# One stage for the parameters, the input norm, the modulation rows and the low-rank inputs, with the row products in four column tiles

## Chip, cores and metric

The kernel runs on one core of one Trainium2 chip. The metric is device microseconds (us) of one execution. TensorE is written PE, VectorE DVE, ScalarE ACT, GpSimd POOL, SyncE SP. A suffix q (SPq) is an engine's own queue of instructions that issue DMAs.

## What is computed

One block with a WKV branch, a state-space branch, a merge and an expert layer. Only its beginning is touched by the change. Cut to that, the reference is:

```python
mod_x = (jax.nn.silu(c) @ w_mod[l] + b_mod[l])[:, None, :]          # w_mod: 2048 x 12288
mod_c = (jax.nn.silu(c_ctx) @ w_mod[l] + b_mod[l])[None, None, :]
sh1x, sc1x, g1x, sh2x, sc2x, g2x = jnp.split(mod_x, N_MOD, axis=-1)
...
hx = rms_norm(x, norm_pre1[l]) * (1.0 + sc1x) + sh1x                # x, ctx: 256 x 2048 each
hc = rms_norm(ctx, norm_pre1[l]) * (1.0 + sc1c) + sh1c
rw_x, z_x, xbc_x, dt_x, gate_x = jnp.split(hx @ w_in[l], IN_SPLITS, axis=-1)
...
# last 640 columns of rw_x, rw_c, after the token shift:
r, k, v, wd_f, wd_b, ad_f, ad_b, gd = jnp.split(slab, RW_SPLITS, axis=-1)   # 96, 96, 96, 96, 256
# used as tanh(wd) @ w2, ad @ a2, sigmoid(gd) @ g2 in the WKV branch
```

Only the first 4096 of the 12288 modulation columns (shift and scale of the first norm) are made in this part; a later stage, which the change leaves alone, makes the rest. All numbers are float32.

## The kernel before

Everything here is laid out with 128 channels on the partitions (P = 128, KC = 16 chunks of channels) and 512 tokens on the free axis (256 of the context, then 256 of x). The order of the work is written out by hand, engine by engine, with semaphores between them. Each stage is a block that all engines enter and leave together. Ahead of the first pair of heads four stages stand one behind the other:

1. setup (lines 166 to 309). SP loads the modulation weights `w_mod_ring`, 8 blocks of 512 columns, 4 MB each, into two buffers. ACT issues 22 small loads of all vectors (`raw`), which PE transposes into `par`. PE then makes one row of 512 modulation values after the other: 16 products (one for each chunk k) with the 128 x 2 `silu_c` as weights and 512 columns of w_mod as the moving side (line 300). So 2 of the array's 128 columns are in use. ACT copies the 2 x 512 row out, PE turns it with 4 small products (line 292, `turn_rows`), and DVE adds the bias (line 271).
2. norm_in (322 to 374). SP loads the token rows (4 x 1 MB), ACT squares them, POOL makes the reciprocal root, DVE scales the rows (line 356), PE transposes them (64 transposes, line 373), and DVE applies gain and shift on the way out of PSUM (line 362), which makes `hT`.
3. lora (380 to 467). SP loads the 5 MB of low-rank input weights `w_lora`. PE runs 6 parts after each other, each over 16 chunks (line 414): 64 products of 96 x 512 and 32 of 128 x 256. ACT and DVE shift each part and apply tanh or sigmoid.
4. The head of rwkv (506 on). SP loads the first weights of the pair loop (`low_rank`, `weights`, `gate_weights`, lines 583 to 596). POOL makes the masks (lines 627 to 652), and ACT, DVE and PE wait for the last of them before the loop over the 16 pairs of heads.

A float32 product stands in the trace as two MATMUL records. The product whose four small ones at a time write partitions 32r to 32r + 31 of one bank (line 1027, in `level_x`) exists in the pair loop:

```python
last = mm(ps[blk(r), 5, q * P:(q + 1) * P], XTc[:, q, blk(r)], F[:, q, r, :], start=True, stop=True)
```

Of the kernel before, what the change touches and what calls it, by code (L numbers as in the profile page):

```python
# [14 lines left out]
ALU = mybir.AluOpType  # L15
# [33 lines left out]
DECAY = -0.6065306597126334  # L49

# [74 lines left out]
def hybrid_block(nc, a, out):  # L125
# [4 lines left out]
    with ExitStack() as whole:  # L130
# [18 lines left out]
        minus_half = sb("minus_half", [P, 1])  # L149
# [16 lines left out]
def setup(nc, sb, sem, ps, a, rows, tiles, ident, ones, head_ones, head_mean, tri, below, minus_half, par, silu_c, modT):  # L166

    with ExitStack() as stage:
        raw = sb("raw", [P, tiles + 1, P], ctx=stage)
        skip = sb("skip", [KC, 2], ctx=stage)  # L170
        sig_c = sb("sig_c", [P, KC, 2], ctx=stage)
        w = sb("w_mod_ring", [P, 2, KC, 512], ctx=stage)
        mod_row = sb("mod_row", [2, 2, 512], ctx=stage)
        consts = sem("consts")
        raw_clear, raw_in = sem("raw_clear"), sem("raw_in")
        w_in = [sem("w_mod_in0"), sem("w_mod_in1")]
        par_tr, par_done, c_sig, c_done = sem("par_tr"), sem("par_done"), sem("c_sig"), sem("c_done")
        skip_done = sem("skip_done")
        row_mm, row_copied, row_tr, mod_done = sem("row_mm"), sem("row_copied"), sem("row_tr"), sem("mod_done")
        w_mod = a["w_mod"].rearrange("l (k p) n -> (l p) k n", p=P)  # L180
        BLOCKS = 2 * D // 512
# [9 lines left out]
        with nc.Block() as block:  # L191

            @block.gpsimd
            def _(pool):
# [12 lines left out]
                const(nc.gpsimd.memset(minus_half[:, :], -0.5))  # L207
                const(nc.gpsimd.memset(ident[:, :], 0.0))
                sel(ident[:, :], ALU.not_equal, 1.0, 0, 1, [[-1, P]])
                const(nc.gpsimd.memset(ones[:, :], 1.0))  # L210
                for t, v in ((head_ones, 1.0), (head_mean, 1.0 / HEAD)):
                    const(nc.gpsimd.memset(t[:, :], 0.0))
                    const(nc.gpsimd.memset(t[0:HEAD, 0:HEAD], v))
                    const(nc.gpsimd.memset(t[HEAD:P, HEAD:P], v))
# [8 lines left out]
                CONSTS[0] = count[0]  # L223

            @block.sync
            def _(sp):
                for n in range(2):
                    sp.dma_start(w[:, n, :, :], w_mod[:, :, n * 512:(n + 1) * 512]).then_inc(w_in[n], 16)
                with sp.Fori(1, BLOCKS // 2) as i:
                    for n in range(2):  # L230
                        sp.wait_ge(row_mm, i * 2 + n - 1)
                        sp.dma_start(w[:, n, :, :],
                                     w_mod[:, :, ds(i * 1024 + n * 512, 512)]).then_inc(w_in[n], 16)

            @block.scalar
            def _(act):
                act.dma_start(skip[:, :], a["ssm_d"].rearrange("l (j e) -> (l j) e", e=2)).then_inc(raw_in, 16)
                act.wait_ge(raw_clear, 1)
                for tile, row, k, width, src in pieces:
                    act.dma_start(raw[row:row + k, tile, 0:width], src).then_inc(raw_in, 16)  # L240
                act.wait_ge(par_done, 2)
                c0 = rows["c"][0]
                for e in range(2):
                    nc.scalar.activation(sig_c[:, :, e], par[:, c0 + e * KC:c0 + (e + 1) * KC],
                                         ACT.Sigmoid).then_inc(c_sig, 1)
                with act.Fori(0, BLOCKS // 2) as i:
                    for n in range(2):
                        act.wait_ge(row_mm, i * 2 + n + 1)
                        nc.scalar.activation(mod_row[:, n, :], ps[0:2, n, :], ACT.Copy).then_inc(row_copied, 1)

            @block.vector
            def _(dve):
# [4 lines left out]
                for half in range(2):  # L257
                    lo, hi = half * 4, min(tiles + 1, half * 4 + 4)
                    dve.wait_ge(par_tr, hi)
                    nc.vector.tensor_copy(par[:, lo * P:hi * P], ps[:, 2 + half, 0:(hi - lo) * P]).then_inc(par_done, 1)  # L260
                dve.wait_ge(c_sig, 2)
                c0 = rows["c"][0]
                for e in range(2):
                    nc.vector.tensor_tensor(silu_c[:, :, e], sig_c[:, :, e], par[:, c0 + e * KC:c0 + (e + 1) * KC],
                                            ALU.mult).then_inc(c_done, 1)
                b0 = rows["b_mod"][0]
                dve.sem_inc(mod_done, 2)
                with dve.Fori(0, BLOCKS // 2) as i:
                    for n in range(2):
                        dve.wait_ge(row_tr, i * 2 + n + 1)  # L270
                        nc.vector.tensor_tensor(
                            modT[:, ds(i * 8 + n * 4, 4), :],
                            ps[:, 4 + n, 0:8].rearrange("p (j e) -> p j e", e=2),
                            par[:, ds(i * 8 + b0 + n * 4, 4)].unsqueeze(2).broadcast_to([P, 4, 2]),
                            ALU.add).then_inc(mod_done, 1)

            @block.tensor
            def _(pe):
                pe.wait_ge(consts, CONSTS[0])
                pe.wait_ge(raw_in, 16 * (len(pieces) + 1))  # L280
                pe.wait_ge(skip_done, 2)
                for t in range(tiles + 1):
                    nc.tensor.transpose(ps[:, 2 + t // 4, (t % 4) * P:(t % 4 + 1) * P], raw[:, t, :],
                                        ident[:, :]).then_inc(par_tr, 1)
                pe.wait_ge(c_done, 2)

                def turn_rows(count, n, guard):

                    pe.wait_ge(row_copied, count + 1)
                    pe.wait_ge(mod_done, guard)  # L290
                    for j in range(4):
                        last = nc.tensor.matmul(ps[:, 4 + n, 2 * j:2 * j + 2], mod_row[:, n, j * P:(j + 1) * P],
                                                ident[0:2, 0:2], start=True, stop=True)
                    last.then_inc(row_tr, 1)

                with pe.Fori(0, BLOCKS // 2) as i:
                    for n in range(2):
                        pe.wait_ge(w_in[n], i * 16 + 16)
                        for k in range(KC):
                            last = nc.tensor.matmul(ps[0:2, n, :], silu_c[:, k, :], w[:, n, k, :],  # L300
                                                    start=(k == 0), stop=(k == KC - 1))
                        last.then_inc(row_mm, 1)
                    for n in range(2):
                        turn_rows(i * 2 + n, n, i * 2 + 2)


CONSTS = [0]


def norm_in(nc, sb, sem, ps, a, ident, minus_half, par, col, modT, hT):  # L310

    with ExitStack() as stage:
        rows = sb("in_rows", [P, NT, D], ctx=stage)
        junk = sb("in_sq", [P, D], ctx=stage)
        ssq = sb("in_ssq", [P, NT], ctx=stage)
        rstd = sb("in_rstd", [P, NT], ctx=stage)
        gain = sb("in_gain", [P, KC, 2], ctx=stage)
        rows_in = [sem(f"rows_in{t}") for t in range(NT)]
        sq_done, rstd_done, gain_done, scaled, turned, h_done = (
            sem(x) for x in ("in_sq_done", "in_rstd_done", "in_gain_done", "in_scaled", "in_turned", "h_done"))  # L320
        srcs = [a["ctx"], a["ctx"], a["x"], a["x"]]
        with nc.Block() as block:

            @block.sync
            def _(sp):
                for t in range(NT):
                    lo = (t % 2) * P
                    sp.dma_start(rows[:, t, :], srcs[t][0, lo:lo + P, :]).then_inc(rows_in[t], 16)

            @block.scalar  # L330
            def _(act):
                for t in range(NT):
                    act.wait_ge(rows_in[t], 16)
                    if t:
                        act.wait_ge(sq_done, t)
                    nc.scalar.activation(junk[:, :], rows[:, t, :], ACT.Square,
                                         accum_out=ssq[:, t:t + 1]).then_inc(sq_done, 1)

            @block.gpsimd
            def _(pool):  # L340
                pool.wait_ge(sq_done, NT)
# [1963 lines left out]
```

## Time and profile before

| | us |
|---|---|
| median of 3 runs | 4772.31 (4768.56 to 4774.83) |
| the profiled execution | 4772.08 |
| its span, first to last instruction | 4770.3 |
| start of the pair loop on PE in it | 297.3 |

The span is shorter than the execution's time by 1.8 us, which lie around it. In the page, a stage is found by its line numbers; in the view of stretches the busy time of an engine is set against the length of the stretch. The mean granted TensorE clock over the span is 0.941 of 2.4 GHz; in a stretch, 1.00 is the upper level and 0.50 the lower (1.2 GHz).

### The profile page before, as it was taken

How to read it: one execution, taken by the hardware profiler on the slowest of the kernel's cores; microseconds unless marked ns; L12 is line 12 of the kernel's file. 1: busy time of each engine (PE TensorE's matmuls, PEld its weight loads, DVE VectorE, ACT ScalarE, POOL GpSimd, SP SyncE). 2: the span in 40 equal slices, each digit the busy share in tenths (PEclk: the TensorE clock that was granted, in tenths of full speed). 3: DMA queues.
4: the chain of work that ended last, by engine and by line, in shares of the span. 5: the costliest groups of instructions: out<-in, count | busy, mean ns of one | idle time of the engine just before them, and what ended most of it. 6: DMA issues, size and time to landing. Idle time of an engine off the chain costs nothing. (4 is left out here: it accounts for less than half of the span.)

```text
span 4770.3 us, 83752 instructions
## 1 busy us (share of the span) xinstructions
PE 4007.9 (84%) x36046; PEld 2453.1 (51%) x36046; DVE 2054.1 (43%) x3479; ACT 732.9 (15%) x1295; POOL 801.7 (17%) x740
## 2 busy tenths in 40 slices
PE   8679999999999967898987999988477777777777
PEld 2246666666666654555655888877332222222233
DVE  0224555555555443656665000011455555545542
ACT  0013222222222211111111000011011011011101
POOL 0020000000000000000100000000354454444441
PEclk9889999999999978889988999999799999999999
DMA  7211111111111105545563443414499999999996
GB/s 270 93 50 42 42 44 43 42 44 43 42 44 43 31 10 158 169 123 149 150 180 100 155 169 143 158 71 150 173 404 400 422 406 406 404 422 402 400 422 260
DMA packets 378768, 868.13 MB, mean 182 GB/s; under 512 B 16300, under 2 KB 211454, under 8 KB 311806
## 3 DMA queue, kind: packets, MB, share of 16 engines
q0 software_dynamic: 73728, 536.90, 27.4%
q1 hardware_dynamic: 303872, 326.74, 22.0%
q8 instruction: 239, 3.92, 0.4%
q10 hardware_dynamic: 894, 0.29, 0.0%
q14 instruction: 35, 0.29, 0.0%
HBM read 859.68 MB, written 4.19 MB: 181 GB/s over the span
## 5 line engine op out<-in xcount | busy, mean ns | idle before, releaser
L2266 PE MATMUL ps<-vb,diag 128*128 128x512 f32 x2048 | 969.8, 621 | 378.5 <-DMA vb<-in_peer_v,ixv 278.8
L2266 PEld LDWEIGHTS ps<-vb,diag 128*128 128x128 f32 x2048 | 384.3, 196 | 964.0 <-issue 606.7
L2168 DVE SCALAR_TENSOR_TENSOR junk<-ub,hT 128x2048 f32<-128x2048 f32 x256 | 586.8, 2292 | 570.4 <-DMA ub<-in_peer_u,ixu 567.9
L945 PE MATMUL ps<-hT,w_pair 128*128 128x512 f32 (+1 forms) x1536 | 661.7, 549 | 37.0 <-POOL id L652 29.8
L1627 PE MATMUL ps<-hT,w_group 128*128 128x512 f32 (+1 forms) x1024 | 404.9, 559 | 19.3 <-DMA w_group<-in_w_in 19.3
L2071 POOL DMA_INDIRECT vb<-in_peer_v,ixv x256 | 311.9, 1218 | 523.4 <-PE ps L2266 485.0
L945 PEld LDWEIGHTS ps<-hT,w_pair 128*128 128x128 f32 x1536 | 261.5, 190 | 189.7 <-issue 130.7
L2063 POOL DMA_INDIRECT ub<-in_peer_u,ixu x256 | 309.0, 1207 | 200.6 <-issue 96.9
L1627 PEld LDWEIGHTS ps<-hT,w_group 128*128 128x128 f32 x1024 | 201.3, 197 | 220.5 <-issue 214.3
L2234 ACT ACTIVATE diag<-ident,coef 128x128 f32<-128x128 f32 x256 | 101.0, 400 | 1007.1 <-PE ps L2266 997.0
L1541 DVE SCALAR_TENSOR_TENSOR mod_by_row<-w_mod_piece,silu_c,mod_by_row 128x512 f32<-128x512 f32 x240 | 187.0, 779 | 114.6 <-DMA w_mod_piece<-in_w_mod 108.9
L1755 PE MATMUL ps<-hT,w_merge 128*128 128x256 f32 x1024 | 223.2, 381 | 14.5 <-DMA w_merge<-in_w_in 14.5
L660 POOL TENSOR_TENSOR bonus<-Kh 128x256 f32<-128x256 f32 x16 | 11.7, 732 | 1223.5 <-DVE Kh L881 1223.5
L1755 PEld LDWEIGHTS ps<-hT,w_merge 128*128 128x128 f32 x1024 | 195.5, 191 | 41.3 <-issue 14.5
L791 DVE SCALAR_TENSOR_TENSOR Ct<-ps,em,Ct 128x64 f32<-128x64 f32 x448 | 106.3, 279 | 185.8 <-PE ps L1044 185.7
L811 DVE TENSOR_TENSOR F<-ps,off 128x1024 f32<-128x1024 f32 x128 | 150.6, 1218 | 61.2 <-PE ps L1019 61.2
L1827 DVE TENSOR_TENSOR sga<-sga,ps 128x1024 f32<-128x1024 f32 x4 | 4.9, 1220 | 339.4 <-PE ps L1755 339.4
L1044 PEld LDWEIGHTS ps<-Ct,Mt 64*64 64x64 f32 x1792 | 73.2, 140 | 116.8 <-issue 87.9
L1454 POOL TENSOR_TENSOR xw<-xt,hd 128x256 f32<-128x256 f32 x48 | 39.6, 857 | 547.9 <-ACT xt L1485 547.9
L1044 PE MATMUL ps<-Ct,Mt 64*64 64x64 f32 x1792 | 104.9, 238 | 13.3 <-DVE Ct L791 13.3
L1936 PE MATMUL ps<-yaT,w_q 128*128 128x256 f32 x512 | 112.5, 383 | 3.3 <-DMA w_q<-in_peer_wq 3.3
L1755 PE MATMUL ps<-mT,w_merge 128*128 128x256 f32 x512 | 112.5, 383 | 2.7 <-DVE mT L1832 2.7
(373 smaller groups left out, 4900.2 us busy)
## 6 DMA issues: line engine op xcount, KB each, us to landing
w_mod_piece<-in_w_mod SPq DMA_DIRECT2D x128, 512.0 KB, 3.8
w_pair<-in_w_in SPq DMA_DIRECT2D x48, 1024.0 KB, 6.0
w_mod_ring<-in_w_mod SPq DMA_DIRECT2D x8, 4096.0 KB, 13.1
w_group<-in_w_in SPq DMA_DIRECT2D x32, 1024.0 KB, 10.6
w_merge<-in_w_in SPq DMA_DIRECT2D x8, 4096.0 KB, 13.2
w_z<-in_w_in SPq DMA_DIRECT2D x8, 2048.0 KB, 13.2
w_merge<-in_w_branch_a SPq DMA_DIRECT2D x4, 4096.0 KB, 13.2
w_merge<-in_w_branch_b SPq DMA_DIRECT2D x4, 4096.0 KB, 13.4
```

The lines of the kernel that those rows point to most:

```text
L791: stt(state(d, c), ps[:, 6, d * HEAD:(d + 1) * HEAD], em[:, z % 2, d, c:c + 1], state(d, c), ALU.mult, ALU.add).then_inc(*VD.did(f"c{j}_{d}"))
L811: tt(F[:, 2 * d:2 * d + 2, :, :], ps[:, 0:4, d * SEQ:(d + 1) * SEQ].rearrange("p r (h c) -> p h r c", h=2), off[:, l - 1, d, :].unsqueeze( ...
L945: last = mm(ps[:, 4, t0:TOK], w[:, m % 2, k, :], hT[:, k, t0:TOK], start=(k == 0), stop=(k == KC - 1))
L1044: last = mm(ps[hs, 6, d * HEAD:(d + 1) * HEAD], m, state(d, before(d, c))[hs, :], start=True, stop=True)
L1541: nc.vector.scalar_tensor_tensor(by_row[:, b, :], part, silu_c[:, k, 0:1], by_row[:, b, :], ALU.mult, ALU.add).then_inc(*DV.did(f"m{m}"))
L1627: last = mm(ps[:, n, t0:TOK], w[:, n, k, :], hT[:, k, t0:TOK], start=(k == 0), stop=(k == KC - 1))
L1755: last = nc.tensor.matmul(ps[:, bank + c // 2, (c % 2) * SEQ:(c % 2 + 1) * SEQ], w[:, slot, k, c * P:(c + 1) * P], rhs[:, k, :], start=(k ...
L1936: last = nc.tensor.matmul(ps[:, 2 * (n % 2) + c // 2, (c % 2) * SEQ:(c % 2 + 1) * SEQ], w[:, n % 2, k, c * P:(c + 1) * P], h2T[:, k, :], s ...
L2063: nc.gpsimd.indirect_dma_start(ub[b][:, :], None, u_tab, bass.IndirectOffsetOnAxis(ap=ixu[:, n, k:k + 1], axis=0)).then_inc(u_in[b], 16)
L2071: nc.gpsimd.indirect_dma_start(vb[b][:, :], None, v_tab, bass.IndirectOffsetOnAxis(ap=ixv[:, n, k:k + 1], axis=0)).then_inc(v_in[b], 16)
L2168: nc.vector.scalar_tensor_tensor(junk[:, :], ub[k % NB][:, :], 1.0, h2_rows[:, n, :], ALU.mult, ALU.mult, accum_out=dots[:, k:k + 1]).then ...
L2266: last = nc.tensor.matmul(ps[:, 4 * n + c, :], diag[:, k % 2, :], vb[k % NB][:, c * 512:(c + 1) * 512], start=False, stop=False)
```

## The change

The four stages become one block, `front`. SP queues the token rows first, then 16 pieces of w_mod (half a row's block each, 2 MB) through a ring of three buffers, with the low-rank weights in four quarters between them, and last the first weights of the pair loop. Two of the four row tiles lie in the buffers of those first weights (`early_rows`).

The modulation row: chunk k goes to column tile k % 4 of PE with 32 columns of weights (two values of `silu_p`, 30 zeros), so that four partial rows stand on partitions 0, 32, 64 and 96; ACT copies all 128 partitions, and the product that turns the row has a 128 x 2 matrix `pick`, which also sums the four. The rows are made in pairs (scale, shift) for 4 chunks of channels. After the transposes ACT copies raw values out of PSUM, and DVE applies gain and shift in place, 4 chunks at a time as their rows come. The low-rank products go chunk by chunk over all six parts (`low_rank`), with the pieces of the next rows between them. POOL makes the reciprocal root first, then all constants and masks. The pair loop and what follows are as before.

```diff
-        setup(nc, sb, sem, ps, a, rows, tiles, ident, ones, head_ones, head_mean, tri, below, minus_half, par, silu_c, modT)
-        norm_in(nc, sb, sem, ps, a, ident, minus_half, par, col, modT, hT)
...
-        rwkv(nc, sb, sem, ps, a, ident, head_ones, head_mean, tri, below, par, col, hT, ya_out, ya_dram)
+        rwkv(nc, sb, sem, ps, a, rows, tiles, ident, ones, head_ones, head_mean, tri, below, par, col, silu_c, modT, hT, ya_out, ya_dram)
...
+        early_rows = w_pair[:, :, :, :].rearrange("p m k c -> p m (k c)")
+        x_rows = [early_rows[:, 0, :], early_rows[:, 1, :], late_rows[:, 0, :], late_rows[:, 1, :]]
+        junk = hT[:, 0:4, :].rearrange("p k t -> p (k t)")
...
+        COLS = [c for b in range(QUARTERS) for c in (D + 512 * b, 512 * b)]
...
+                def mod_piece(q):
+                    if q >= 3:
+                        sp.wait_ge(piece_mm, q - 2)
+                    c0, k0 = COLS[q // 2], q % 2 * (KC // 2)
+                    sp.dma_start(ring[:, q % 3, :].rearrange("p (k n) -> p k n", n=512),
+                                 w_mod[:, k0:k0 + KC // 2, c0:c0 + 512]).then_inc(piece_in[q % 3], 16)
+
+                def lora_weights(b):
+                    sp.dma_start(w[:, 4 * b:4 * b + 4, :], w_src[:, 4 * b:4 * b + 4, L0:RW_COLS]).then_inc(w_in, 16)
+
+                srcs = [a["ctx"], a["ctx"], a["x"], a["x"]]
+                for n in range(NT):
+                    lo = (n % 2) * P
+                    sp.dma_start(x_rows[n], srcs[n][0, lo:lo + P, :]).then_inc(rows_in[n], 16)
+                for q in range(3):
+                    mod_piece(q)
+                lora_weights(0)
+                for b in range(QUARTERS):
+                    for q in range(4 * b + 3, min(4 * b + 7, 16)):
+                        mod_piece(q)
+                    if b + 1 < QUARTERS:
+                        lora_weights(b + 1)
+                sp.wait_ge(turned, KC)
+                first_weights(sp)
...
+                pool.wait_ge(sq_done, NT)
+                nc.gpsimd.tensor_scalar(rstd[:, :], ssq[:, :], 1.0 / D, EPS, ALU.mult, ALU.add).then_inc(rstd_done, 1)
+                pool.wait_ge(rstd_done, 1)
+                nc.gpsimd.tensor_tensor(rstd[:, :], rstd[:, :], half[:, 0:1].broadcast_to([P, NT]), ALU.pow).then_inc(rstd_done, 1)
+                pool.wait_ge(rstd_done, 2)
...
+                const(nc.gpsimd.memset(pad_rw[:, :, :, :], 0.0))
...
+                pool.wait_ge(piece_mm, 4 * QUARTERS)
...
+                for n in range(NT):
+                    act.wait_ge(rows_in[n], 16)
+                    if n:
+                        act.wait_ge(sq_done, n)
+                    nc.scalar.activation(junk, x_rows[n], ACT.Square, accum_out=ssq[:, n:n + 1]).then_inc(sq_done, 1)
...
+                def copy_row(m):
+                    act.wait_ge(piece_mm, 2 * m + 2)
+                    if m >= 2:
+                        act.wait_ge(row_tr, m - 1)
+                    nc.scalar.activation(mod_row[:, m % 2, :], ps[:, 6, :], ACT.Copy).then_inc(row_copied, 1)
+
+                copy_row(0)
+                act.wait_ge(sq_done, NT)
+                for j in range(KC):
+                    act.wait_ge(turned, j + 1)
+                    nc.scalar.activation(hT[:, j, :], ps[:, 2 + j % 4, :], ACT.Copy).then_inc(h_raw, 1)
+                for m in range(1, 2 * QUARTERS):
+                    copy_row(m)
...
+                def add_bias(m):
+                    j = COLS[m] // P
+                    dve.wait_ge(row_tr, m + 1)
+                    nc.vector.tensor_tensor(modT[:, j:j + 4, :], ps[:, 7, 0:8].rearrange("p (j e) -> p j e", e=2),
+                                            par[:, b0 + j:b0 + j + 4].unsqueeze(2).broadcast_to([P, 4, 2]), ALU.add).then_inc(mod_done, 1)
+
+                for b in range(QUARTERS):
+                    j = 4 * b
+                    add_bias(2 * b)
+                    dve.wait_ge(mod_done, 2 * b + 1)
+                    nc.vector.scalar_tensor_tensor(gain[:, j:j + 4, :], modT[:, KC + j:KC + j + 4, :], 1.0,
+                                                   par[:, g0 + j:g0 + j + 4].unsqueeze(2).broadcast_to([P, 4, 2]),
+                                                   ALU.add, ALU.mult).then_inc(gained, 1)
+                    add_bias(2 * b + 1)
+                    dve.wait_ge(mod_done, 2 * b + 2)
+                    dve.wait_ge(gained, b + 1)
+                    for k in range(j, j + 4):
+                        dve.wait_ge(h_raw, k + 1)
+                        for s, e in ((0, 1), (1, 0)):
+                            nc.vector.tensor_scalar(hT[:, k, s * SEQ:(s + 1) * SEQ], hT[:, k, s * SEQ:(s + 1) * SEQ],
+                                                    gain[:, k, e:e + 1], modT[:, k, e:e + 1], ALU.mult, ALU.add).then_inc(h_done, 1)
...
+                def row_piece(q):
+                    m, k0 = q // 2, q % 2 * (KC // 2)
+                    pe.wait_ge(piece_in[q % 3], 16 * (q // 3 + 1))
+                    if q % 2 == 0 and m:
+                        pe.wait_ge(row_copied, m)
+                    for k in range(k0, k0 + KC // 2):
+                        g = k % 4
+                        last = mm(ps[32 * g:32 * g + 32, 6, :], silu_p[:, k, :], ring[:, q % 3, (k - k0) * 512:(k - k0 + 1) * 512],
+                                  start=(k < 4), stop=(k >= KC - 4))
+                    last.then_inc(piece_mm, 1)
+
+                def turn_row(m):
+                    pe.wait_ge(row_copied, m + 1)
+                    if m:
+                        pe.wait_ge(mod_done, m)
+                    for j in range(4):
+                        last = mm(ps[:, 7, 2 * j:2 * j + 2], mod_row[:, m % 2, j * P:(j + 1) * P], pick[:, :], start=True, stop=True)
+                    last.then_inc(row_tr, 1)
+
+                def low_rank(n, k):
+                    c, m, t0 = parts[n]
+                    pe.wait_ge(h_done, 2 * k + 2)
+                    last = mm(ps[0:m, n, t0:TOK], w[:, k, c:c + m], hT[:, k, t0:TOK], start=(k == 0), stop=(k == KC - 1))
+                    if k == KC - 1:
+                        last.then_inc(proj, 1)
+
+                row_piece(0)
+                row_piece(1)
+                pe.wait_ge(scaled, NT)
+                for j in range(KC):
+                    if j >= 4:
+                        pe.wait_ge(h_raw, j - 3)
+                    for n in range(NT):
+                        last = nc.tensor.transpose(ps[:, 2 + j % 4, n * P:(n + 1) * P], x_rows[n][:, j * P:(j + 1) * P], ident[:, :])
+                    last.then_inc(turned, 1)
+                turn_row(0)
+                row_piece(2)
+                row_piece(3)
+                turn_row(1)
+                pe.wait_ge(h_raw, KC)
+                pe.wait_ge(par_done, 2)
+                for b in range(QUARTERS):
+                    pe.wait_ge(w_in, 16 * (b + 1))
+                    if b < QUARTERS - 1:
+                        row_piece(4 * b + 4)
+                        for k in range(4):
+                            for n in range(6):
+                                low_rank(n, 4 * b + k)
+                            if k < 3:
+                                row_piece(4 * b + 5 + k)
+                            if k == 1:
+                                turn_row(2 * b + 2)
+                            if k == 3:
+                                turn_row(2 * b + 3)
+                    else:
+                        for n in range(6):
+                            for k in range(4):
+                                low_rank(n, 4 * b + k)
```

In the following lists names on the left of the arrow are written, those on the right read; xN is N instructions in a row. On PE, from the vectors' transposes to the start of the pair loop, before:

```order
L283 MATMUL ps<-ident,raw 128x128 x6
L296 UNCONDITIONAL_BRANCH
L296 ISA
L300 MATMUL ps<-w_mod_ring,silu_c 2x512 x32
L289 ISA
L290 REGISTER_ALU
L292 MATMUL ps<-ident,mod_row 128x2 x8
```

These are one turn of a loop that is passed four times; all row products come ahead of the token transposes. Now, on PE behind the token transposes (L486), up to the second chunk's low-rank products:

```order
L469 MATMUL ps<-pick,mod_row 128x2 x4
L460 MATMUL ps<-w_mod_ring,silu_p 32x512 x16
L469 MATMUL ps<-pick,mod_row 128x2 x4
L460 MATMUL ps<-w_mod_ring,silu_p 32x512 x8
L475 MATMUL ps<-hT,w_lora 96x512 x4
L475 MATMUL ps<-hT,w_lora 128x256 x2
L460 MATMUL ps<-w_mod_ring,silu_p 32x512 x8
L475 MATMUL ps<-hT,w_lora 96x512 x4
L475 MATMUL ps<-hT,w_lora 128x256 x2
```

Pieces of rows (8 products) now stand between the low-rank products of each chunk (6 products). On ACT, from the last small load to the copies of the transposes, now:

```order
L326 DMA raw<-in_c_ctx 16x128
L331 ACT_TABLE_LOAD
L331 ACTIVATE hT,in_ssq<-w_pair 128x2048 x2
L331 ACTIVATE hT,in_ssq<-in_rows 128x2048 x2
L335 ACT_TABLE_LOAD
L335 ACTIVATE sig_c<-par 128x16 x2
L341 ACTIVATE mod_row<-ps 128x512
L347 ACTIVATE hT<-ps 128x512 x16
```

The four squares moved ahead of the sigmoid of c, with a table load ahead of each kind. On SP, from the token rows to the first weights of the pair loop, now:

```order
L235 DMA w_pair<-in_ctx 128x2048 x2
L235 DMA in_rows<-in_x 128x2048 x2
L226 DMA w_mod_ring<-in_w_mod 128x8x512 x3
L230 DMA w_lora<-in_w_in 128x4x640
L226 DMA w_mod_ring<-in_w_mod 128x8x512 x4
L230 DMA w_lora<-in_w_in 128x4x640
```

The last two rows come twice more before the last piece and the first weights; each piece from the fourth on waits for the piece three before it to be used.

## Rows read from the trace of the kernel before

**Rows 1.** The page, its head:
```profile
span 4770.3 us, 83752 instructions
```
**Rows 2.** Stretches: from:to, length, busy us (instructions), clock, DMA share, GB/s.
```profile
0.00:23.30 23.30, 1.52 (x7) 1.15 (x7) 1.57 (x6) 1.60 (x3) 6.05 (x25) 1.00 0.96 336
23.30:142.40 119.10, 119.09 (x320) 28.98 (x320) 1.17 (x7) 4.69 (x8) 0.00 (x0) 1.00 0.60 218
142.40:164.70 22.30, 0.03 (x1) 0.04 (x1) 5.23 (x6) 8.01 (x8) 1.25 (x2) 0.57 0.48 189
164.70:177.60 12.90, 11.11 (x64) 9.04 (x64) 11.70 (x26) 0.00 (x0) 0.00 (x0) 0.82 0.00 0
177.60:197.00 19.40, 0.02 (x1) 0.02 (x1) 7.09 (x23) 0.00 (x0) 3.63 (x2) 0.55 0.72 271
197.00:267.50 70.50, 70.46 (x192) 33.43 (x192) 6.65 (x10) 5.41 (x10) 0.00 (x0) 0.98 0.00 0
267.50:297.30 29.80, 0.00 (x0) 0.00 (x0) 0.91 (x2) 2.39 (x6) 23.19 (x57) 0.57 0.33 82
```
**Rows 3.** Timeline of PE: start, us, what, [idle before, releaser].
```profile
23.30 28.93 PE L300 MATMUL ps<-w_mod_ring,silu_c 128*2 128x512 f32 x64 [1.52 <-DVE silu_c L264]
52.16 1.94 PE L292 MATMUL ps<-ident,mod_row 2*128 2x2 f32 x16
54.03 27.63 PE L300 MATMUL ps<-w_mod_ring,silu_c 128*2 128x512 f32 x64
...
196.98 70.48 PE L414 MATMUL ps<-hT,w_lora 128*96 128x512 f32 x192 [19.43 <-DMA w_lora<-in_w_in]
297.30 11.38 PE L945 MATMUL ps<-hT,w_pair 128*128 128x512 f32 x20 [29.84 <-POOL id L652]
```
**Rows 4.** Timeline of PE in the pair loop, one of 64 such products' groups.
```profile
623.79 1.08 PE L1027 MATMUL ps<-F,XTc 128*32 128x128 f32 x32
624.80 1.13 PE L945 MATMUL ps<-hT,w_pair 128*128 128x512 f32 x2
```
**Rows 5.** Timeline of ACT and DVE in setup.
```profile
11.32 1.28 ACT L244 ACT_TABLE_LOAD   x1 [11.32 <-issue]
19.83 0.28 DVE L255 COPY raw<-skip 16x64 f32<-16x64 f32 x2 [19.83 <-DMA raw<-in_c_ctx]
22.80 0.26 DVE L264 TENSOR_TENSOR silu_c<-sig_c,par 128x16 f32<-128x16 f32 x2 [0.39 <-ACT sig_c L244]
```
**Rows 6.** Timeline of ACT and DVE in norm_in.
```profile
148.80 1.91 ACT L336 ACTIVATE in_sq<-in_rows 128x2048 f32<-128x2048 f32 x1 [7.66 <-DMA in_rows<-in_ctx]
...
156.27 1.91 ACT L336 ACTIVATE in_sq<-in_rows 128x2048 f32<-128x2048 f32 x1 [0.48 <-DMA in_rows<-in_x]
...
159.74 4.87 DVE L356 TENSOR_SCALAR in_rows<-in_rows,in_rstd 128x2048 f32<-128x2048 f32 x4 [16.41 <-POOL in_rstd L344]
165.90 14.56 DVE L362 TENSOR_SCALAR hT<-ps,in_gain,modT 128x256 f32<-128x256 f32 x32 [1.29 <-PE ps L373]
```
**Rows 7.** Stretches in which DMA is the busiest: setup, its later loads, w_lora, first weights.
```profile
4.00:20.00 16.00, 0.00 (x0) 0.00 (x0) 0.17 (x2) 1.28 (x1) 3.39 (x10) 1.00 1.06 371
...
88.00:92.00 4.00, 4.00 (x10) 0.77 (x9) 0.00 (x0) 0.00 (x0) 0.00 (x0) 1.00 1.05 386
186.00:194.00 8.00, 0.00 (x0) 0.00 (x0) 0.00 (x0) 0.00 (x0) 0.00 (x0) 0.50 1.03 400
277.00:281.00 4.00, 0.00 (x0) 0.00 (x0) 0.00 (x0) 0.00 (x0) 3.47 (x8) 0.50 1.18 283
```
**Rows 8.** Timeline at the end of lora and of the masks, ACT and POOL.
```profile
212.57 0.59 ACT L425 ACTIVATE lora_pad<-ps 96x512 f32<-96x512 f32 x1 [54.29 <-PE ps L414]
...
269.17 0.71 ACT L435 ACTIVATE gate_g<-lora_near 128x256 f32<-128x256 f32 x2
...
270.15 1.39 POOL L627 MEMSET pad<- 128x1548 f32 x1 [85.72 <-POOLq L397]
...
296.73 0.53 POOL L652 COPY id<-ident 64x64 f32<-64x64 f32 x2
```

More of the change, by code:

```diff
@@ L163, in hybrid_block @@
         peer(nc, sb, sem, ps, a, out, ident, ones, par, col, modT, hT, yaT, ybT, xT)
-def setup(nc, sb, sem, ps, a, rows, tiles, ident, ones, head_ones, head_mean, tri, below, minus_half, par, silu_c, modT):
-    with ExitStack() as stage:
[L169 to L176, printed above, removed]
-        par_tr, par_done, c_sig, c_done = sem("par_tr"), sem("par_done"), sem("c_sig"), sem("c_done")
-        skip_done = sem("skip_done")
-        row_mm, row_copied, row_tr, mod_done = sem("row_mm"), sem("row_copied"), sem("row_tr"), sem("mod_done")
+CONSTS = [0]
@@ L222, in _ @@
                         sel(below[:, d, e, :], ALU.is_ge, 0.0, base, -sign, [[sign, P]])
[L223 to L233, printed above, removed]
+                const(nc.gpsimd.memset(pad_rw[:, :, :, :], 0.0))
@@ new lines, in _ @@
+                const(nc.gpsimd.memset(em[:, :, :, :], 0.0))
+                const(nc.gpsimd.memset(ln_eps[:, :], LN_X_EPS))
+                const(nc.gpsimd.memset(blocks[:, :, :], 1.0))
+                for n in range(5):
+                    b = 2 << n
+                    v = blocks[:, n, :].rearrange("p (j b) -> p j b", b=b)
+                    for base, cm, step in ((0, 1, -b), (b - 1, -1, b)):
+                        const(nc.gpsimd.affine_select(out=v, in_=v, compare_op=ALU.is_ge, fill=0.0, base=base,
+                                                      pattern=[[step, P // b], [0, b]], channel_multiplier=cm))
@@ new lines, in _ @@
+                const(nc.gpsimd.tensor_tensor(tri[:, :, :, :].rearrange("p d e t -> p (d e) t"), tri[:, :, :, :].rearrange("p d e t -> p (d e) t"),
+                                              blocks[:, 4, :].unsqueeze(1).broadcast_to([P, 4, P]), ALU.mult))
+                for l in range(1, 5):
+                    for d in range(2):
+                        const(nc.gpsimd.tensor_tensor(off[:, l - 1, d, :], blocks[:, l - 1, :], blocks[:, l, :], ALU.subtract))
+                        const(nc.gpsimd.tensor_tensor(off[:, l - 1, d, :], off[:, l - 1, d, :], below[:, 1 - d, 0, :], ALU.mult))
@@ new lines, in _ @@
+                for r in range(4):
+                    rs = slice(r * CH, (r + 1) * CH)
+                    wide = lambda m, n: m.unsqueeze(1).broadcast_to([CH, n, CH])
+                    four = lambda m: m.rearrange("p (n c) -> p n c", c=CH)
+                    for d in range(2):
+                        const(nc.gpsimd.tensor_copy(four(strict[rs, d, :]), wide(below[rs, d, 0, rs], 4)))
+                        const(nc.gpsimd.tensor_copy(four(incl[rs, d, :]), wide(below[rs, d, 1, rs], 2)))
+                    const(nc.gpsimd.tensor_copy(four(id32[rs, :]), wide(ident[rs, rs], 4)))
+                    const(nc.gpsimd.tensor_scalar(four(neg2[rs, :]), wide(blocks[rs, 0, rs], 4), -1.0, None, ALU.mult))
@@ L261, in _ @@
                 dve.wait_ge(c_sig, 2)
+                dve.wait_ge(consts, CONSTS[0])
                 c0 = rows["c"][0]
                 for e in range(2):
[L264 to L304, printed above, removed]
@@ L495, in need, with rwkv @@
         engine.wait_ge(*marks.by(name, pair))
-CH = 32
-NC = TOK // CH
-def rwkv(nc, sb, sem, ps, a, ident, head_ones, head_mean, tri, below, par, col, hT, ya_out, ya_dram):
+def rwkv(nc, sb, sem, ps, a, rows, tiles, ident, ones, head_ones, head_mean, tri, below, par, col, silu_c, modT, hT, ya_out, ya_dram):
     with ExitStack() as stage:
@@ L643, in _ @@
-                for r in range(4):
-                    wide = lambda m, n: m.unsqueeze(1).broadcast_to([CH, n, CH])
-                    four = lambda m: m.rearrange("p (n c) -> p n c", c=CH)
-                    for d in range(2):
-                        const(nc.gpsimd.tensor_copy(four(strict[blk(r), d, :]), wide(below[blk(r), d, 0, blk(r)], 4)))
-                        const(nc.gpsimd.tensor_copy(four(incl[blk(r), d, :]), wide(below[blk(r), d, 1, blk(r)], 2)))
-                    const(nc.gpsimd.tensor_copy(four(id32[blk(r), :]), wide(ident[blk(r), blk(r)], 4)))
-                    const(nc.gpsimd.tensor_scalar(four(neg2[blk(r), :]), wide(blocks[blk(r), 0, blk(r)], 4), -1.0, None, ALU.mult))
@@ L651, in _ @@
-                for h in range(2):
-                    const(nc.gpsimd.tensor_copy(id64[head(h), :], ident[head(h), head(h)]))
-                MASKS[0] = count[0]
                 for i in turns:
```

312 lines of the change are left out of this document (125 added, 187 removed).

## The prediction

> **What bounds the kernel now.** I read four views, from coarse to fine. The page gives the span, 4770.3 us [rows 1]. The view of stretches, cut where PE's line numbers change, shows that the four stages ahead of the pair loop lie end to end [rows 2]: PE is busy without a gap from 23.3 to 142.4 and from 197.0 to 267.5, and next to idle in the four stretches around them, 0 to 23.3, 142.4 to 164.7, 177.6 to 197.0 and 267.5 to 297.3. DMA is at full rate only where PE idles, or by turns. So the place is bound by order. PE's timeline names each end of waiting [rows 3]: silu_c at 23.30, the load of w_lora at 196.98 (19.43 us of waiting), the last mask of POOL at 297.30 (29.84 us). The pair loop cannot begin before, and nothing behind 297.30 is edited, so the change is worth what it moves that start (call it T), and nothing else.
>
> **Part 1, row products.** One record of 512 columns takes 27.63/64 = 0.432 us at the upper clock [rows 3]. 8 blocks x 16 products x 2 records = 256 records, 110.5 us, all on the path. In column tiles, four products are to run at once. The nearest row is line 1027: 16 products of 128 columns on four column tiles, 32 records, begin at 623.79, and the next wide product begins 1.01 us later [rows 4]. One after another, 32 records of 128 columns are 32 x 0.432/4 = 3.45 us; at a quarter 0.86, so 0.15 us goes to the change of shape. One piece (8 products, 16 records of 512) is then 16 x 0.432/4 + 0.15 = 1.88 us; without overlap it is 16 x 0.432 + 0.15 = 7.06. I take 1.88, since line 1027 has the same 128 partitions of moving data, four tiles and one bank.
>
> Those rows were also the reason to weigh a rule. The Trainium skill, TensorEngine Tiling (Array Packing), Key Properties, says that a change of tiling mode drains TensorE, which speaks against pieces set between wide products. The trace puts it within the 0.15 us above, and 16 pieces of it are 2.4 us, which are in the sum.
>
> **Part 2, the low-rank products** are the same 192 records: 128 of 512 and 64 of 256 columns, (128 + 32) x 0.432 = 69.1 us; the row has 70.48, with 1.4 lost to the low clock after the wait [rows 3]. Per chunk 4.32 us, per quarter 17.3. **Turning a row** costs 1.94/2 = 0.97 us of PE as before (four products, their weights still 128 wide).
>
> **Part 3, the start.** The last small load comes in at 19.83, the first product starts at 23.30 [rows 3, 5]. Now ACT squares first: its DMAs are issued by 11.3, a table load of 1.28 follows [rows 5], then the squares, 148.80 to 158.18, 9.4 us [rows 6], until 22.0; then a second table load, 23.3, the sigmoids and four small DVE operations (two took 0.26, rows 5): first product at 24.2. Behind the small loads there is more risk: they share the DMA engines with the token rows, whose contiguous pieces are larger than those of w_mod. I add 1.5 us, between 0 and 4. DVE scales the rows 4.87 us behind the silu [rows 6], 29.2, beside the first two pieces on PE. Those cost 2 x 1.88 and 1.3 for the low clock of a start (28.93 against 27.63, rows 3): 29.3. Even.
>
> The 64 transposes are paced by what empties PSUM. DVE's exit took 14.56/16 = 0.91 us a chunk [rows 6]; ACT now copies, 0.59 us for such a tile [rows 8]. I take 0.6 x 16 = 9.6, at most 14.6: 38.9. Then turn, two pieces, 43.6; PE waits for ACT's copy, 0.9; turn, 45.5.
>
> **Part 4, steady state.** Three quarters of 4 pieces, 4 chunks and 2 turns: 4 x 1.88 + 17.3 + 1.94 = 26.8 us each, 125.9. In the last there is no piece to hide the bias, gain and first chunk on DVE behind the last turn: 1.4, then 17.3: 144.6. The end of lora, from PE's last record (267.46) to the next block's first instruction (270.15), is 2.7 [rows 3, 8]; 0.3 to PE's start. With the 1.5 of Part 3, **T = 149**.
>
> **What hides what.** Masks: POOL needs 296.73 + 0.53 - 270.15 = 27 us [rows 8] and 6 us of constants [rows 2]; they start at 23.5 and are waited for at 149, with 90 us to spare. First weights: SP issues them behind the last piece; from 270.15, they and the masks were done by 297.3 in any case. The first weights are behind the last piece's wait (`piece_mm` 13, about 100 us), and nobody waits for them before T. ACT's copy of a row lies under the next chunk's products. If DVE's work in place of the exit was 2 x as slow as PSUM's 0.455 us a half chunk, a quarter would take 7.3 us of 26.8: hidden.
>
> **DMA.** The queue carries 4.2 + 33.6 + 5.2 = 43.0 MB, 9.7 MB a quarter (4 x 2.10 + 1.31). Full rate was 371 with the small loads, 386 later, 400 for w_lora [rows 7]. At 386, 25.1 us a quarter, under PE's 26.8. With three buffers, piece q leaves when q - 3 is used; following this through, each piece is there 2 to 4 us before its products. So PE sets the pace, narrowly. The Trainium skill, DMA: Bandwidth & Descriptors, Bandwidth, puts the limit for HBM at about 358 GB/s for a core; the loads of w_mod at 386 are above it, so here the measurement decides. By the page's figure, as an estimate, a quarter would take 27.1 us, and T would be some 4 us later; that is within the second case below.
>
> **The sum.** 297.3 - 149 = 148.3 us earlier. The pair loop's first 20 records took 11.38 us, against 20 x 0.432 = 8.64, after 29.8 us of idleness [rows 3]; now PE idles 3 us ahead of them. I take the whole 2.7, bounds 0 and 2.7. 4770.3 - 151.0 + 1.8 around the span (4772.08 against 4770.3) = **4621 us**, 3.2% less; the median of before is only 0.2 above the profiled execution.
>
> **Rivals.**
> - A, as summed: 4621, within 4611 and 4632 (transposes +5, small loads -1.5 to +2.5, clock +2.7, semaphores). Chance 0.70.
> - B, DMA sets the pace: pieces late because each waits for a buffer. At the 336 GB/s of the first stretch [rows 2] the last piece is in at 130 us, and 28.9 us follow (piece, chunk, turn, 1.4, 17.3, 3.0): T = 159, 4631. At the 283 of the worst pattern, the 512-byte pieces of w_pair [rows 7], it is in at 154: T = 183, 4655. For it: the margin is 7%. Against: w_mod itself had 386. Chance 0.19.
> - C, the tiles take turns: 16 x 5.18 = 83 us more, T = 232, 4704. Two at a time: 16 x 1.73 = 28 more, 4649. Against: line 1027. Chance 0.07.
> - D, the change holds the clock down in the block, since PE stops at each late piece: all of PE's work doubled, 69 + 28 us more, T = 246, some 4718. Against: clock 1.00 throughout the 2-column products [rows 2]. Chance 0.025.
> - E, slower than before: a product on 32 columns neither overlaps with others nor lifts the clock, 8 x 1.73 = 13.8 us a piece, 16 x 11.9 = 191 more, T = 340, 4812. It decides from (297.3 + 2.7 - 149)/16 + 1.88 = 11.3 us a piece. Against: line 1027, and that twice. Chance 0.015. That the masks or the first weights still come last would need 90 us more of POOL, and is in the same 0.015.
>
> **How the numbers follow.** The likeliest is A, 4621. The range takes A and most of B, with the mild half of C: 4611 to 4652, about 0.1 left out above and little below. Within 0.2% (9.5 us, about what a measurement of this kernel tells from no change) only a blend of D and E could end: 0.01. Faster 0.975, same 0.01, slower 0.015.
>
> **What would show it.** In the profile of after: PE's first product of the pair loop at 149 (T itself). Row products: a group of 16 records 1.9 us long; 7 us would be C. Stretches of 26.8 us a quarter with PE busy all over and DMA share near 0.95; gaps ahead of row products released by w_mod_ring are B. Clock 1.00 from 30 us on; 0.5 is D. Transposes in 10 us, released by ACT. First row product at 24 to 26; if the small loads come in later than 22, Part 3's 1.5 was too small. POOL's last mask before 70. Stages behind T, shifted and otherwise of equal length: if they changed by over 3 us, the argument that only T counts is wrong.

## The result: 3.2% less, and where the two traces part

| | us |
|---|---|
| before, 4 runs beside it | 4770.44 (4764.37 to 4774.83) |
| after, 4 runs | 4619.22 (4615.69 to 4620.4) |
| ratio | 0.9682, 95% interval 0.967 to 0.9695 |
| forecast | 4621, range 4611 to 4652 |
| the profiled execution of after, its span | 4620.4, 4618.7 |
| T, start of the pair loop, before and after | 297.30, 150.79 |

Nearly the whole gain is T: 146.5 of the 151.6 us between the two profiled spans. The timeline of PE in the kernel after shows how the merged stage runs. As in [rows 3], the columns are start, us, what and count, and in brackets the idle time before and what ended it:

```profile
25.26 4.92 PE L460 MATMUL ps<-w_mod_ring,silu_p 128*32 128x512 f32 x32 [1.43 <-DVE silu_p L382]
30.84 0.44 PE L486 MATMUL ps<-ident,w_pair 128*128 128x128 f32 x2 [0.66 <-DVE in_rows L386]
...
38.13 0.95 PE L469 MATMUL ps<-pick,mod_row 128*128 128x2 f32 x8
39.01 3.86 PE L460 MATMUL ps<-w_mod_ring,silu_p 128*32 128x512 f32 x32
43.59 1.05 PE L469 MATMUL ps<-pick,mod_row 128*128 128x2 f32 x8 [0.72 <-ACT mod_row L341]
46.67 3.64 PE L460 MATMUL ps<-w_mod_ring,silu_p 128*32 128x512 f32 x16 [2.03 <-DMA w_mod_ring<-in_w_mod]
50.25 5.29 PE L475 MATMUL ps<-hT,w_lora 128*96 128x512 f32 x12
55.47 1.92 PE L460 MATMUL ps<-w_mod_ring,silu_p 128*32 128x512 f32 x16
57.32 4.54 PE L475 MATMUL ps<-hT,w_lora 128*96 128x512 f32 x12
...
131.24 17.40 PE L475 MATMUL ps<-hT,w_lora 128*96 128x512 f32 x48 [1.12 <-DVE hT L429]
150.79 10.51 PE L954 MATMUL ps<-hT,w_pair 128*128 128x512 f32 x20 [2.16 <-PEq L218]
```

Line 460 is the row products, 486 the transposes, 469 the turning of a row, 475 the low-rank products. A piece of eight products takes 57.32 - 55.47 = 1.85 us. From 46.67, where piece 4 begins (pieces are counted from 0), until the last turn is done, at 130.1, PE waits for nobody. The two long waits of [rows 3], 19.43 and 29.84 us, are gone. The only wait on DMA is the one that ends at 46.67, and the piece behind it takes 3.58 us instead of 1.85.

The stretches of after (from:to, length, busy us of PE, PEld, DVE, ACT, POOL, clock, DMA share, GB/s) give the reason for both:

```profile
40.00:45.00 5.00, 3.91 (x36) 1.41 (x28) 0.28 (x2) 0.60 (x1) 4.32 (x10) 1.00 1.04 383
45.00:50.00 5.00, 3.33 (x16) 0.69 (x16) 4.08 (x8) 0.00 (x0) 4.29 (x10) 0.50 1.05 387
85.00:90.00 5.00, 5.00 (x23) 2.00 (x25) 0.00 (x0) 0.02 (x1) 0.00 (x0) 1.00 1.05 387
120.00:125.00 5.00, 5.00 (x26) 1.88 (x25) 0.00 (x0) 0.07 (x1) 0.00 (x0) 1.00 0.84 230
```

DMA is full at about 387 GB/s, which it was only here and there in [rows 7]; the pace it sets stays just ahead of PE's. In the wait the granted clock falls to its lower level: it is 0.97 from 44.5 to 45.0 and 0.50 from 45.0 to 45.5, so it fell some 0.3 us after the wait began at 44.64. It stays at 0.50 through piece 4 and is back at 1.00 from 52 us on. The masks that ended at 297.3 in [rows 8] now end at 60.6, in POOL's timeline:

```profile
60.08 0.53 POOL L316 COPY id<-ident 64x64 f32<-64x64 f32 x2
```

### The profile page after: what moved, and what is told of

The parts are those of the page before. It is cut to its first block and busy times, and to the rows that moved or that the text cites. A ratio compares the mean times of both kernels' runs of the same rounds, so it can differ in the third digit from the quotient of the medians.

```text
span 4618.7 us, 83699 instructions
## 1 busy us (share of the span) xinstructions
PE 3930.4 (85%) x36046; PEld 2440.8 (53%) x36046; DVE 2051.2 (44%) x3484; ACT 743.0 (16%) x1312; POOL 793.7 (17%) x747
## 5 line engine op out<-in xcount | busy, mean ns | idle before, releaser
L2078 POOL DMA_INDIRECT vb<-in_peer_v,ixv x256 | 297.9, 1164 | 528.9 <-PE ps L2273 505.3
L1638 PE MATMUL ps<-hT,w_z 128*128 128x256 f32 x512 | 113.2, 379 | 0.0
```

Of the source, the lines that this page charges most:

```text
L1638: last = mm(ps[:, 4, e * SEQ:(e + 1) * SEQ], wz[:, k, e * P:(e + 1) * P], hT[:, k, SEQ:TOK], start=(k == 0), stop=(k == KC - 1))
L2078: nc.gpsimd.indirect_dma_start(vb[b][:, :], None, v_tab, bass.IndirectOffsetOnAxis(ap=ixv[:, n, k:k + 1], axis=0)).then_inc(v_in[b], 16)
```

## The experiments

Theory 1, from the prediction: PE's chain sets the merged stage, four tiles make a piece 1.88 us long, the masks are worth 27 us and the first weights some 6. Rivals: the row products overlap less than the sum says, or DMA sets the pace, so that PE's gain is lost to it. Each kernel is after with one edit, except `before_tiles`, which starts from before, and turn_early, which adds an edit to piece_first. T is read from one profiled execution of each kernel; that of the unedited kernel came out at 150.79 and 150.60. The medians of before beside them were 4772.9 to 4774.8.

| kernel | median us | ratio, 95% | T |
|---|---|---|---|
| one_tile | 4697.1 | 0.9836, 0.982 to 0.9852 | 229.57 |
| two_tiles | 4640.01 | 0.9724, 0.9708 to 0.974 | 175.13 |
| masks_late | 4652.39 | 0.9747, 0.973 to 0.9763 | 177.84 |
| weights_late | 4627.91 | 0.9685, 0.9669 to 0.9702 | 156.89 |
| before_tiles | 4735.58 | 0.9923, 0.9905 to 0.9942 | 258.06 |
| piece_first | 4616.3 | 0.9668, 0.9653 to 0.9684 | 147.96 |
| after_again (unedited) | 4620.43 | 0.9671, 0.9658 to 0.9684 | 150.60 |
| turn_early | 4615.07 | 0.9662, 0.9649 to 0.9675 | 146.91 |
| light_pe (one run) | 4604.65 | | 143.75 |
| rows_second (one run) | 4631.68 | | 156.17 |

### Are the tiles what makes a piece short? one_tile and two_tiles

```diff
-                        g = k % 4
+                        g = k % 1
...
-                                  start=(k < 4), stop=(k >= KC - 4))
+                                  start=(k < 1), stop=(k >= KC - 1))
```

> All row products on one column tile (32 columns of weights, partitions 0 to 31), nothing else changed. Theory 1 (the four tiles overlap and PE paces the new stage): each of 16 pieces costs 7.0 us instead of 1.86, the pair loop starts 83 us later (at 234), about 4702 us. Theory 2 (DMA paces the stage anyway, DMA being busy at 387 GB/s to 115 us in the trace of after): part of the 83 us is hidden, under 4670 us.

two_tiles has `k % 2` and 2 in the same places. In both, ACT's copy of a row and the products that turn it take only the partitions in use, 32 or 64.

> Row products on two column tiles instead of four. Theory 1 (overlap goes with the number of tiles, PE paces): 16 x 1.73 = 28 us later, 4647 us. Theory 2 (DMA paces): within 10 us of the changed kernel, under 4630 us.

A full piece and the chunk behind it, PE's timeline of one_tile:

```profile
65.53 7.05 PE L460 MATMUL ps<-w_mod_ring,silu_p 128*32 128x512 f32 x16
72.51 4.54 PE L475 MATMUL ps<-hT,w_lora 128*96 128x512 f32 x12
...
229.57 8.82 PE L954 MATMUL ps<-hT,w_pair 128*128 128x512 f32 x20 [2.16 <-PEq L218]
```

The same of two_tiles:

```profile
52.20 3.63 PE L460 MATMUL ps<-w_mod_ring,silu_p 128*32 128x512 f32 x16
55.76 4.54 PE L475 MATMUL ps<-hT,w_lora 128*96 128x512 f32 x12
```

The same instructions take 6.98, 3.56 and 1.85 us from start to start on one, two and four tiles. For n tiles that is 6.84/n + 0.14 us, so 0.14 us a piece doesn't shrink with the tiles. A fit of two terms to three times can't say what the 0.14 us is. T is 78.8 and 24.3 us later than in after. By the pieces it would be 16 x 5.13 = 82 and 16 x 1.71 = 27; in both kernels the wait for piece 4 and its low clock, 4.5 us in after, are absent, because PE comes later. Against that, the first two pieces, whose first records take twice their later time in every kernel, take 16.65 and 9.92 us, which exceeds two full pieces by 1.5 and 1.6 us more than in after. The expectations, 4702 and 4647, were 5 and 7 us too high.

### The masks and the first weights: masks_late and weights_late

masks_late puts all of POOL's masks back at the head of the pair loop's block, with the waits for them.

```diff
-                const(nc.gpsimd.memset(pad_rw[:, :, :, :], 0.0))
...
             def _(pool):
+                count = [0]
...
+                const(nc.gpsimd.memset(pad[:, :, :, :], 0.0))
```

> The masks of the pair loop are made again at the head of the pair loop's block, and waited for there; the rest as in the changed kernel. Theory (the masks were the last arrival ahead of the pair loop and are fully hidden now): 27 us of POOL come back, and up to 2 us for a clock at the low level behind the pause: 4646 to 4649 us. Rival (the hidden masks slow DVE in the new stage, so leaving them out there gives something back): under 4643 us.

```diff
-                sp.wait_ge(turned, KC)
-                first_weights(sp)
...
+                first_weights(sp)
                 for i in turns:
```

> The first weights of the pair loop are loaded at the head of its block instead of in the new stage. Theory: the first 1 MB load needs 6 us to land, so the pair loop starts 6 us later, 4625 us. Rival (the load's time is hidden behind the entry of the block): 4619 us.

PE's timeline of masks_late, the pair loop's first record:

```profile
177.84 2.93 PE L967 MATMUL ps<-hT,w_pair 128*128 128x512 f32 x3 [29.27 <-POOL id L674]
```

and of weights_late:

```profile
156.89 11.05 PE L953 MATMUL ps<-hT,w_pair 128*128 128x512 f32 x20 [8.31 <-DMA w_pair<-in_w_in]
```

T is 27.1 and 6.1 us later, each released by what was moved. That the masks slow the merged stage, the rival, doesn't show: PE is done with it at 148.57 without them and at 148.63 with them. The medians move by more than T, 33.2 and 8.7 us over that of after; the four runs of masks_late lie between 4639.84 and 4654.91, and T stands for the lowest of them only. So 4652.39 missed the 4646 to 4649 that I had expected, and the part behind T is too variable to say more from the medians. In before the load lay wholly under the masks, so that it cost nothing there; with the masks moved alone it should come to the surface, which no kernel here shows, and the 6.1 us say what it costs then.

### The tiles without the merging: before_tiles

before, with the four column tiles in setup (and the `silu_p`, `pick` and copy of 128 partitions that they need) and nothing else of the change.

```diff
-                            last = nc.tensor.matmul(ps[0:2, n, :], silu_c[:, k, :], w[:, n, k, :],
-                                                    start=(k == 0), stop=(k == KC - 1))
+                            g = k % 4
+                            last = nc.tensor.matmul(ps[32 * g:32 * g + 32, n, :], silu_p[:, k, :], w[:, n, k, :],
+                                                    start=(k < 4), stop=(k >= KC - 4))
```

> The kernel before with one edit: its row products on four column tiles; the stages stay one behind the other. Theory (setup then runs at the pace of its loads, 8 x 4.19 MB at 387 GB/s = 87 us): setup ends at 96 instead of 142, about 4725 us, so the tiles alone give a third of the whole gain. Rival (setup's loads keep up with PE): 16 x 5.2 = 83 us less, about 4688 us.

PE's timeline of it:

```profile
42.41 6.44 PE L309 MATMUL ps<-w_mod_ring,silu_p 128*32 128x512 f32 x32 [8.00 <-DMA w_mod_ring<-in_w_mod]
53.25 6.14 PE L309 MATMUL ps<-w_mod_ring,silu_p 128*32 128x512 f32 x32 [4.40 <-DMA w_mod_ring<-in_w_mod]
...
101.46 1.95 PE L300 MATMUL ps<-pick,mod_row 128*128 128x2 f32 x16
```

and one stretch, columns as above:

```profile
60.00:96.00 36.00, 19.77 (x124) 6.72 (x123) 0.67 (x4) 1.86 (x4) 0.00 (x0) 0.76 1.04 384
```

T falls by 39.2 us only, and I had expected 46: I had ended setup with its last load, but the last block's products begin at 96.55 and they and the turn last until 103.4. Setup now runs at the pace of its loads: 33.6 MB at 386 GB/s are 87 us, whatever PE does. All six later blocks wait for their load, 2.8 to 8.0 us each, and 32 records take 5 to 6.4 us instead of 3.7, with the granted clock at 0.76 in the mean from 60 to 96. So the tiles are worth 39 us alone and 79 in the merged stage, where the low-rank products stand in the time in which the loads run.

### Does DMA set the pace behind PE? light_pe

It leaves out 60 of the 96 low-rank products, about 42 us of PE (12 chunks at 4.47 us, of which 0.93 us each stays).

```diff
-                            for n in range(6):
-                                low_rank(n, 4 * b + k)
+                            low_rank(0, 4 * b + k)
```

> Leaves out 60 of the 96 low-rank products (five of the six parts for the first 12 of 16 chunks), so that TensorE has 41 us less to do in the new stage while the loads stay the same. Theory 1 (TensorE paces the stage, with much room on DMA): the pair loop starts 41 us earlier, at 109. Theory 2 (DMA is close behind: 43 MB at 387 GB/s are in at 113 us, and 25 us of work follow the last piece): it starts at 138, only 13 us earlier, with waits for w_mod_ring ahead of the row products.

PE's timeline and one stretch of it:

```profile
91.35 3.64 PE L460 MATMUL ps<-w_mod_ring,silu_p 128*32 128x512 f32 x16 [4.89 <-DMA w_mod_ring<-in_w_mod]
...
116.34 3.25 PE L460 MATMUL ps<-w_mod_ring,silu_p 128*32 128x512 f32 x16 [4.94 <-DMA w_mod_ring<-in_w_mod]
...
143.75 8.82 PE L953 MATMUL ps<-hT,w_pair 128*128 128x512 f32 x20 [2.15 <-PEq L218]
```

```profile
45.00:100.00 55.00, 37.27 (x194) 11.33 (x194) 10.66 (x31) 2.39 (x4) 13.36 (x38) 0.81 1.05 388
```

Five eighths of the low-rank products gone bring T only 7.0 us forward. Of the twelve pieces from piece 4 on, ten wait, up to 4.94 us, and six run wholly or partly at the lower clock, so that they take 2.9 to 3.6 us instead of 1.85. T missed both expectations, 109 and 138, and is near the second: the last piece's products begin at 116.3 and 27.4 us follow, where I had 113 and 25. Rival B was thus close behind A: PE sets the pace in after, but the loads would set almost the same one.

### Order in the queue: piece_first, turn_early, rows_second

piece_first queues the first quarter of the low-rank weights behind piece 4, gives each quarter a semaphore of its own, and lets PE wait for it behind piece 4's products.

```diff
-                lora_weights(0)
                 for b in range(QUARTERS):
...
                         mod_piece(q)
+                        if q == 4:
+                            lora_weights(0)
```

> The first quarter of low-rank weights is queued behind piece 4 instead of ahead of piece 3, and PE waits for it behind that piece's products. Theory (in the trace of after PE waits 2.0 us for piece 4, and the granted clock is 0.50 behind that gap, which makes piece 4 take 3.6 instead of 1.9 us and the next chunk 5.2 instead of 4.5): the gap and the low clock go, the pair loop starts 4.5 us earlier (at 146), about 4615 us. Rival (the wait moves on to the low-rank weights, and the clock still falls): no difference, 4619 us.

turn_early adds to it that the second row of a pair is turned in the middle of the quarter's last chunk, so that bias, gain and DVE's shift are ready when PE needs them.

```diff
                                 low_rank(n, 4 * b + k)
+                                if k == 3 and n == 2:
+                                    turn_row(2 * b + 3)
...
-                            if k == 3:
-                                turn_row(2 * b + 3)
```

> The first quarter of low-rank weights behind piece 4, as in piece_first, and each second row of a pair turned in the middle of its quarter's last chunk instead of behind it. Theory: the gap and low clock at 45 us go (2.8 us in piece_first) and the wait of 1.1 us ahead of the last quarter goes: the pair loop starts at 147, about 4 us under the changed kernel, 4615 us. Rival (PE waits as long for ACT's copy of the row): 148, no difference to piece_first.

> The changed kernel, unchanged, beside the next one on one chip. Theory (in the trace of after the clock fell behind the gap of 2.2 us at the pair loop's start, while behind the same gap in two other kernels it did not: chance): the pair loop starts at 149 to 151, its first 20 records take 8.8 or 10.5 us, 4619 us.

PE's timeline of piece_first:

```profile
44.13 1.92 PE L462 MATMUL ps<-w_mod_ring,silu_p 128*32 128x512 f32 x16
...
51.65 1.92 PE L462 MATMUL ps<-w_mod_ring,silu_p 128*32 128x512 f32 x16 [0.88 <-DMA w_mod_ring<-in_w_mod]
...
66.18 1.92 PE L462 MATMUL ps<-w_mod_ring,silu_p 128*32 128x512 f32 x16 [0.92 <-DMA w_mod_ring<-in_w_mod]
...
147.96 8.82 PE L957 MATMUL ps<-hT,w_pair 128*128 128x512 f32 x20 [2.15 <-PEq L219]
```

The wait of 2.03 us and its low clock are gone, but I had expected 4.5 us and T gave 2.8: in a full queue a wait that is removed comes back in smaller ones, 0.18, 0.88 and 0.92. Of these none brought the clock down. turn_early starts the pair loop at 146.91, where 147 was expected, and is the only kernel in which PE's wait for DVE ahead of the last quarter is gone too; beside after_again, on the same chip, its T is 3.7 us earlier and its median 5.4 us less. The two intervals overlap, so that it isn't shown to be better in time, only in the T of one execution each.

rows_second queues three pieces of w_mod ahead of the token rows.

> The first three pieces of w_mod are queued ahead of the token rows. Theory 1 (the small loads came in 2.1 us later than before because the token rows' contiguous pieces are larger than those of w_mod and share the DMA engines): DVE starts at 19.8 again; the token rows come later and the pair loop starts about 7 us later, at 158. Theory 2 (it is not the kind of load beside them): DVE's start stays at 21.9.

DVE's timeline of rows_second, the last small load:

```profile
19.95 0.28 DVE L371 COPY raw<-skip 16x64 f32<-16x64 f32 x2 [19.95 <-DMA raw<-in_c_ctx]
```

and of after:

```profile
21.89 0.28 DVE L371 COPY raw<-skip 16x64 f32<-16x64 f32 x2 [21.89 <-DMA raw<-in_c_ctx]
```

With the token rows behind, the small loads are in at 19.95, as in before (19.83, [rows 5]); beside them, at 21.89. The Trainium skill, DMA: Bandwidth & Descriptors, Queues, rings and completion order, says that an engine takes turns between queues packet by packet; that fits, though these runs don't show packets. The order is no gain all the same: ACT's squares then wait for the token rows, the first row product comes at 35.79, and T is 5.4 us later.

## Why the prediction was right

**The argument that T alone counts** held in substance. The part behind T took 4473.0 us in before and 4467.9 in after, 5.1 less, of which 11.38 - 10.51 = 0.9 is the first 20 records of the pair loop. I had written that a change of over 3 us would refute it. That bound was too tight: in after_again, the same kernel as after, the same part took 4473.3, and over all ten kernels it lies between 4457.2 and 4473.7.

**The steps of the sum**, with the 1.5 of Part 3 put where it arose:

| step | predicted | measured |
|---|---|---|
| first row product | 25.7 | 25.26 |
| transposes, start to end | 30.8 to 40.4 | 30.84 to 38.13 |
| second turn done | 47.0 | 44.6 |
| wait for piece 4 | 0 | 2.03 |
| three quarters | 80.4 | 29.4 + 27.0 + 27.0 |
| DVE's wait, idle time of PE | 1.4 | 1.12 |
| last quarter | 17.3 | 17.40 |
| end of lora to the pair loop | 3.0 | 2.16 |
| T | 149 | 150.79 |

- Part 1 held: 1.85 us a piece against 1.88, and tiles don't take turns. By the rule on mode switches of the Trainium skill, TensorEngine Tiling (Array Packing), Key Properties, something had to be lost; the three tile runs allow 0.14 us a piece for it, about the 0.15 of the prediction, and don't show that it is this.
- Part 2, a chunk between two pieces, was too small: it takes 4.47 us from start to start, in one_tile and two_tiles as in after, where its records alone come to 4.32. That is why the quarters are 27.0 and not 26.8, and what it is stays open.
- Part 3, small loads: 2.06 us later, not 1.5. The first row product still came 0.4 us early, since I had put the second table load into the chain, while it began before the last small load was in and ended at 22.55, ahead of the parameters that the sigmoid waits for:

```profile
21.27 1.28 ACT L335 ACT_TABLE_LOAD   x1
24.50 0.32 ACT L335 ACTIVATE sig_c<-par 128x16 f32<-128x16 f32 x2 [1.95 <-DVE par L376]
31.60 7.95 ACT L347 ACTIVATE hT<-ps 128x512 f32<-128x512 f32 x16 [0.74 <-PE ps L486]
```

- Part 3, first two pieces: 4.92 us, 1.2 over two full ones, where I took 1.3 for the low clock of a start. The size held, but the granted clock reads 1.00 from 25 to 31 in after, as it does in the first rows of [rows 2], so that no row shows the clock to be the cause.
- Part 3, transposes: their start, 30.84 for 30.8, is luck: DVE began the rows 0.5 us earlier and took 5.6 us for them instead of 4.87, which nearly cancels. The last row of ACT's timeline is the exit, 7.95/16 = 0.50 us each. I took 0.6 from [rows 8], a copy that stands alone; alone, a 128 x 512 copy takes 0.60 us in after too (line 341). The term was 2.3 us too large.
- **The step that failed** is in the paragraph on DMA, "each piece is there 2 to 4 us before its products". Up to piece 4 the queue carries 4.2 MB of token rows, five pieces and a quarter of w_lora, 16.0 MB; at 386 GB/s 41.4 us, from some 5 us on: 46.5, and it was 46.67. My own chain wanted it at 47.0, so even there only 0.3 us was to spare, and not 2 to 4. In after_again and weights_late piece 3 was 0.4 us late as well. PE came 2.4 us earlier than planned and gave 2.0 back in the wait; in it the clock fell, and piece and chunk took 1.7 + 0.8 = 2.5 us more. The steps' errors, unrounded, add up to +1.7: -2.4, +2.0, +3.0 in the quarters, -0.3, +0.1, -0.8. The prediction's estimate for a lower rate, T some 4 us later, was not summed as B was: by B's formula it is T = 151, 2 us later.
- The clock gain at the pair loop's start was 0.9 us, where I took the whole of 2.7. T and this term left the time 3.6 us above the forecast, and the variation behind T took it back. So a miss of 1.8 us is partly luck; the bounds around A were right in size.

**The shares.** Undone one at a time, the tiles are worth 79 us of T, the masks 27, the first weights 6, together 112 of 146.5. The 34.5 that remain belong to the merging itself (norm_in and the load of w_lora under other work); that is a remainder and was not run alone. The shares depend on the rest, as before_tiles shows for the largest.

## What to carry over

Find the first instruction that the change leaves alone, and sum only what moves it; here that put four stages into one number. For each load in a full queue, the bytes ahead of it over the measured rate say when it can be there at the earliest: set that beside the chain of the engine that wants it, one load after another, since the average over a quarter hides the first. A faster product is worth its time only where something else can run while its data come: 39 us alone, 79 in company.

## What the runs showed beside that

- **A short gap at times halves the clock.** Ahead of the pair loop PE idles 2.15 us in eight of these kernels. Its first 20 records then took 10.5 us in after, after_again and turn_early and 8.82 in one_tile, two_tiles, piece_first, light_pe and rows_second: up to 1.7 us that no edit explains. The gaps of 0.7 and 1.9 to 2.2 us around one turned row ahead of piece 4, on the other hand, were followed by the lower clock in after, after_again, masks_late and weights_late, and for part of the piece in light_pe (0.72 and 1.79, then 2.93 us): in all that had them. In the first four the clock fell 0.3 to 1.1 us after the second gap began, in light_pe only within the piece behind it, so the length of that gap alone doesn't decide it.
- **Waits on loads feed themselves.** In before_tiles and light_pe the clock stood at 0.76 and 0.81 in the mean over 36 and 55 us, so that PE took up to 1.9 times as long for a piece, with time that the next load then used. Why some waits of 2.5 us brought the clock down and others did not stays open.
